# A decoder step with paged attention: the first decode sequence scored in another order, two key pages turned into a free buffer, and the last turn of the output moved by one tile

## The reference

```python
q = rms_norm((xn @ fox_w_q).reshape(B, T, H_B, HEAD_DIM), fox_q_norm)
# prompt: 256 rows attend causally to themselves
# decode sequence b: 8 rows attend to 8 cached pages of 128 rows, and to the 8 new rows
s = einsum('bqhd,bkhd->bhqk', q, k) / 8 + f_q - f_k      # masked by position
p = softmax(s); o = einsum('bhqk,bkhd->bqhd', p, v)
h = h + o.reshape(B, T, 1024) @ fox_w_o
```

## Time and profile before

| | us |
|---|---|
| median of 3 runs | 1571.27 |
| lowest and highest | 1570.28, 1572.79 |
| the profiled execution's own time | 1571.32 |
| its span in the trace | 1569.3 |
| PE busy | 1521.4 (97%) |
| DVE busy | 966.0 (62%) |
| ACT busy | 663.1 (42%) |
| projection `q` ends, attention begins (span's clock) | 1131 |
| output projection begins | 1288.7 |

### The profile page before, as it was taken

The page is one execution under the profiler, slowest core; times in us unless marked ns, Lnnn a source line. Parts: engine busy times, 40 slices in busy tenths (PEclk is TensorE's granted clock), DMA queues, the critical chain, the costliest instruction groups (busy, mean ns, idle before and its releaser), DMA issues.

```text
span 1569.3 us, 34147 instructions
## 1 busy us (share of the span) xinstructions
PE 1521.4 (97%) x14068; PEld 1420.4 (91%) x14068; DVE 966.0 (62%) x1394; ACT 663.1 (42%) x1029; POOL 125.4 (8%) x183
## 2 busy tenths in 40 slices
PE   8999999999999999999999999999988879999998
PEld 8999998998888799999999999999845549999998
DVE  6655446686897576554458655544688865655532
ACT  5443333663655653434344333333334444443321
POOL 0000000002331300000000432000012210000000
PEclk9999999999999999999999999999999999999999
DMA  8766673440010466657774554444979993444442
GB/s 267 238 213 204 223 222 106 135 135 16 17 30 10 136 204 225 226 189 228 228 240 149 180 167 142 148 148 155 376 281 408 407 367 121 135 160 137 151 148 81
DMA packets 241004, 288.54 MB, mean 184 GB/s; under 512 B 18898, under 2 KB 221922, under 8 KB 240754
## 3 DMA queue, kind: packets, MB, share of 16 engines
q1 hardware_dynamic: 237234, 281.20, 53.1%
q0 software_dynamic: 3648, 5.57, 1.4%
HBM read 280.39 MB, written 39.90 MB: 204 GB/s over the span
## 4 chain that ended last, share of the span: by engine, by line
PE 85%; DVE 9%; ACT 2%; issue 2%; DMA 1%; SPq 0%; POOL 0%; DVEq 0%
PE ps L758 24%; PE ps L759 23%; PE ps L760 23%; PE ps L1059 4%; PE ps L1054 3%; DVE ring L2841 1%; DVE ring_r L2240 1%; DMA ring<-in_fox_w_o 1%; PE ps L1511 1%; PE ps L1085 1%; PE ps L1194 1%; PE ps L1210 1%; PE ps L1149 1%; ACT ring L1882 0%; ACT ring_r L1703 0%
## 5 line engine op out<-in xcount | busy, mean ns | idle before, releaser
L758 PE MATMUL ps<-arena_r,ring_r 128*128 128x320 f32 (+1 forms) x2024 | 627.2, 310 | 0.0
L760 PE MATMUL ps<-arena_r,ring_r 128*128 128x320 f32 (+1 forms) x2024 | 624.6, 309 | 0.0
L2240 DVE TENSOR_TENSOR ring_r<-ring,ring_r 128x2048 fp32r<-128x2048 f32 (+2 forms) x131 | 291.4, 2226 | 256.8 <-ACT ring_r L1703 152.3
L758 PEld LDWEIGHTS ps<-arena_r,ring_r 128*128 128x128 f32 x2024 | 381.1, 188 | 4.1 <-issue 3.4
L760 PEld LDWEIGHTS ps<-arena_r,ring_r 128*128 128x128 f32 x2024 | 381.0, 188 | 0.0
L759 PE MATMUL ps<-arena_r,ring_r 128*128 128x320 f32 x1136 | 351.0, 309 | 0.0
L759 PE MATMUL ps<-xn_r,ring_r 128*128 128x320 f32 (+2 forms) x888 | 273.6, 308 | 0.0
L759 PEld LDWEIGHTS ps<-arena_r,ring_r 128*128 128x128 f32 x1136 | 213.3, 188 | 0.2
L2240 DVE TENSOR_TENSOR arena_r<-arena,arena_r (+3 forms) x155 | 142.2, 928 | 112.1 <-ACT arena_r L1703 50.1
L758 PE MATMUL ps<-arena_r 128*128 128x320 f32 x592 | 183.2, 309 | 0.0
L760 PE MATMUL ps<-arena_r 128*128 128x320 f32 x592 | 182.9, 309 | 0.0
(11 more groups left out here) (381 smaller groups left out, 1830.1 us busy)
## 6 DMA issues: line engine op xcount, KB each, us to landing
ring<-in_ffn_w_in SPq DMA_DIRECT2D x66, 1024.0 KB, 5.1
k_grouped<-in_cache_k SPq DMA_DIRECT2D x64, 512.0 KB, 5.4
ring<-in_ffn_w_out SPq DMA_DIRECT2D x24, 1024.0 KB, 5.1
arena<-in_cache_v SPq DMA_DIRECT2D x45, 512.0 KB, 9.4
ring<-k_grouped SPq DMA_DIRECT2D x44, 512.0 KB, 8.5
arena<-in_ffn_w_in SPq DMA_DIRECT2D x21, 1024.0 KB, 5.1
ring<-in_rw_w_rkv SPq DMA_DIRECT2D x11, 1024.0 KB, 5.1
arena<-k_grouped SPq DMA_DIRECT2D x20, 512.0 KB, 8.7
```

Of the source, the lines that this page charges most:

```text
L758: pe.matmul(out, part(s, 1)[:, k, cs], x_hi, start=first_, stop=False)
L760: return pe.matmul(out, part(s, 0)[:, k, cs], x_hi, start=False, stop=last)
L2240: return TT(out, x, high.bitcast(F32), ALU.subtract)
```

## The change

In words, for each engine:

- **Tiles.** `k_own` gets its bank before the four `q_rep` tiles. With that `q_rep` no longer occupies a bank of sequence 1's scores, and sequence 0 uses those two banks (`SCORES[1]`) for its own keys' scores and for its turned probabilities.
- **DVE.** Pages 4 and 5 of sequence 0 (unit 2) are turned into `xn`, whose content is no longer needed, so they need not wait for a scored unit: page 4 before the first `query_reciprocal`, page 5 before the mask. From unit 3 on the two buffers of `k_feat` alternate one step later. `prompt_scaled` comes after `less_max(0)`, and page 8 (the first of sequence 1) before `own_max(0)`. The steps for sequence 1 are written out: page pairs, `fox_scored(1)`, `fox_sums`, and the scaled output of sequence 0 before the last pair of pages; `less_max(1)` before `fox_scored(2)`.
- **PE.** `k_own`, units 2 and 3 and the own keys before `query_rep("q_rep")`; `fox_scores(0)` after the turned probabilities; `unit_scores(1, 2)` before `fox_values(0)`, `turn_output(0)` before `unit_scores(1, 3)`.
- **ACT.** For sequence 0 `probability_copy` before `fox_exp(0)`.
- **Output projection.** PE does the first rows of tile 1 before `turn_output(7)` instead of after it. DVE does `scaled_output(7)` before the low part of slab `fo` + 1 instead of after it.

Nothing is added to or taken from the work. The diff, shortened where a block only repeats the words above:

```diff
     add("q_own", 1, "a")
+    add("k_own", 1, "a")
     add("q_rep", DT // 2)
-    add("k_own", 1, "a")
...
-        OWN = P_TURNED[1]
+        def own_bank(b):
+            return P_TURNED[1] if b else SCORES[1][1]
         def turned(b):
-            return P_TURNED if b < BS - 1 else SCORES[(b + 1) % 2]
+            return P_TURNED if 0 < b < BS - 1 else SCORES[(b + 1) % 2]
+        def key_unit(n):
+            return xn_f[:, 0:2 * D] if n == 2 else k_feat[(n - 1) % 2 if n > 2 else n]
...
             unit_scores(0, 0)
             unit_scores(0, 1)
+            head_groups("k_own", kT)
             pe.wait_ge(S("q_rn"), 2)
+            unit_scores(0, 2)
+            unit_scores(0, 3)
+            own_scores(0)
             query_rep("q_rep", P, 2, rs[:, TS:TS + P])
-            head_groups("k_own", kT)
-            unit_scores(0, 2)
-            own_scores(0)
-            unit_scores(0, 3)
-            fox_scores(0)
...
             turn_probabilities(0)
+            fox_scores(0)
+            pe.wait_ge(S("pT_ready"), 1)
             unit_scores(1, 0)
...
+            dve_done(first["q_rep"] + 3)
             own_scores(1)
             fox_turn(1)
+            unit_scores(1, 2)
             fox_values(0)
-            unit_scores(1, 2)
+            turn_output(0)
+            unit_scores(1, 3)
             fox_scores(2)
-            unit_scores(1, 3)
-            turn_output(0)
             fox_scores(3)
...
             first_outputs(0, slice(0, T - P))
+            first_outputs(1, slice(0, T - P))
             pe.wait_ge(S("o_out"), 2 * (BS - 1))
             turn_output(b)
-            first_outputs(1, slice(0, T - P))
             split(first_slab["fo"] + 1)
...
-            for b in range(1, 5):
+            exps(0)
+            probability_copy(0)
+            fox_exp(0)
+            past_forget(1, 1)
...
-                if unit >= 2:
-                    dve.wait_ge(S("unit_scored"), unit - 1)
+                if unit >= 3:
+                    dve.wait_ge(S("unit_scored"), unit - 2 if unit < 5 else unit - 1)
...
             dve.wait_ge(dve_freed, freed["d"][first["q"] + DT])
+            turn_page(0, 4)
             query_reciprocal("q_norm_s", 0, TS)
...
             query_reciprocal("q_norm", TS, P)
+            turn_page(0, 5)
...
-            for j in range(4, PAGES):
-                turn_page(0, j)
+            turn_page(0, 6)
+            turn_page(0, 7)
             half_max(0)
-            prompt_scaled(0)
-            prompt_scaled(1)
-            prompt_scaled(2)
+            turn_page(1, 0)
             own_max(0)
-            prompt_scaled(3)
             less_max(0)
-            turn_page(1, 0)
+            for g in range(4):
+                prompt_scaled(g)
             turn_page(1, 1)
             fox_scored(0)
...
             probability_sums(b)
+            scaled_output(b)
             lo(first_slab["fo"] + 1)
-            scaled_output(b)
```

More of the change, by code:

```diff
@@ L1398, in turn_probabilities @@
             def turn_probabilities(b):
-                if b == 0:
-                    dve_done(first["q_rep"] + 3)
                 if b == BS - 1:
@@ L1506, in unit_scores @@
                               start=(j == 0), stop=False, is_transpose=True, skip_group_check=True)
-                keys = k_feat[u % 2].rearrange("p (n f x u) -> p x n f u", n=2, f=4, x=DT)
+                keys = key_unit(b * 4 + u).rearrange("p (n f x u) -> p x n f u", n=2, f=4, x=DT)
                 for e in range(2):
@@ L1524, in own_scores @@
                         x = 2 * c + e
-                        mm = mmul(ps[32 * c:32 * c + 32, OWN, 0:TS], q_cur[b % 2][:, x * 32:x * 32 + 32],
+                        mm = mmul(ps[32 * c:32 * c + 32, own_bank(b), 0:TS], q_cur[b % 2][:, x * 32:x * 32 + 32],
                                   kT[:, x, TP:T], e == 0, e == 1)
@@ L2156, in exps @@
                 own_exp(b)
-            for b in range(1, 5):
+            exps(0)
+            probability_copy(0)
+            fox_exp(0)
+            past_forget(1, 1)
+            fox_exp(1)
+            fox_columns(0)
+            fox_columns(1)
+            fox_out(0)
+            past_forget(2, 0)
+            output_columns(0)
+            for b in range(2, 5):
                 exps(b - 1)
@@ L2837, in turn_page @@
                 unit = (b * PAGES + j) // 2
-                if unit >= 2:
-                    dve.wait_ge(S("unit_scored"), unit - 1)
+                if unit >= 3:
+                    dve.wait_ge(S("unit_scored"), unit - 2 if unit < 5 else unit - 1)
                 dve.wait_ge(*k_page_in(b, j))
-                dve.transpose(k_feat[unit % 2][:, j % 2 * D:(j % 2 + 1) * D], k_page(b, j)).then_inc(S("page_turned"), 1)
+                dve.transpose(key_unit(unit)[:, j % 2 * D:(j % 2 + 1) * D], k_page(b, j)).then_inc(S("page_turned"), 1)
             def query_reciprocal(name, c0, n):
@@ L2920, in own_max @@
                     dve.wait_ge(S("p_row"), b * 3)
-                link(TT(s_new, ps[:, OWN, 0:TS], mask_new[:, b, :], ALU.add))
+                link(TT(s_new, ps[:, own_bank(b), 0:TS], mask_new[:, b, :], ALU.add))
                 dve.tensor_reduce(sst[:, 2:3], s_new, AX.X, ALU.max)
@@ L2961, in turn_pages @@
                 turn_page(b, j + 1)
-            for b in range(1, 4):
+            turn_pages(1, 2)
+            fox_scored(1)
+            fox_sums(0)
+            turn_pages(1, 4)
+            fox_sums(1)
+            probability_sums(0)
+            scaled_output(0)
+            turn_pages(1, 6)
+            half_max(1)
+            own_max(1)
+            turn_pages(2, 0)
+            less_max(1)
+            fox_scored(2)
+            fox_scored(3)
+            for b in range(2, 4):
                 turn_pages(b, 2)
-                if b == 1:
-                    fox_scored(1)
                 fox_sums(2 * b - 2)
```

## The result

The changed kernel takes 1562.69 us (median of 5 runs, 1557.42 to 1564.12), the kernel before 1571.27 (5 runs beside them); the ratio is 0.9949, with a 95% interval of 0.9931 to 0.9968. In the experiments the changed kernel was measured once more: 1561.42 us (8 runs, 1557.6 to 1564.74) against 1570.94 us, ratio 0.9939 (0.9921 to 0.9956). The forecast was 1562.4 us. Single executions of both kernels and of some variants that took far longer (1654 to 3746 us) are in no median and no ratio.

A forecast was written before the change was run, and what follows sets the result against it. PE was busy 1521.4 of 1569.3 us; the attention was paced by DVE and PE in turn and by the transfers. From 1571.3 us, 6.4 (end) plus 2.5 (front), 8.9 in all, gave 1562.4 us, range 1560.5 to 1566.5.

The forecast's parts named there:

- gain at the end: Last value page to last rows' matmuls: 6.4 us won, 4.0 of it PE's wait before `turn_output(7)`, the rest clock.
- slab `fo` + 1 in front of tile 2: Output projection: the slab's low part is ready just after PE asks for it for tile 2, a 0.1 us wait.
- page 4's cost: Sequence 0 on DVE: turning page 4 before the first reciprocal delays scaling, queries and first unit by 0.4 us.
- last value page on PE: End of the attention: the last value page's landing moves 2.5 us earlier, from 1287.5 to 1285.0 us.
- The rival of the whole half: End: all 6.83 us at 1.2 GHz give back half, 3.4 us; end 7.4, kernel 1561.4 us; chance 0.05.
- The smaller of the two shifts arrives: Attention: transfers shift by 2.5 us, DVE and PE by 3.3; only the smaller, 2.5, reaches the last value page.
- end alone: Rival: the front's gain is absorbed and only the end's 6.4 us arrives, 1564.9 us; chance 0.11.
- The slab's rival: Output projection: slab `fo` + 1 still lands at 1290.2, tile 2 waits for it, 1564.9 us; chance 0.08.
- The engines' shift: Sequence 1: DVE and PE run 3.3 us earlier than before, DVE's row at 1172.34 coming at 1169.0.
- the wait on DMA: Sign of being right: PE still waits on DMA at the last value page, near 1.4 us, before 0.65.
- The new wait: Sequence 1 on PE: `fox_scores(3)` waits some 2.2 us because `fox_scored(2)` follows `less_max(1)`; priced at nothing.
- The slower case: Rival: new waits drop the clock to 1.2 GHz in four new stretches, 1576 us; slower or nothing has chance 0.02.

The follow-up runs named there:

- the front alone: The changed kernel with its two moves in the output projection (`first_outputs(1)` on PE, `scaled_output(7)` on DVE) undone; 1567.39 us, ratio 0.9977 to the kernel before.
- the end alone: The kernel before with only the two output projection moves (`first_outputs(1)` before `turn_output(7)`, `scaled_output(7)` before the low part of slab `fo` + 1); 1564.44 us, ratio 0.9957.
- the scaling first: The changed kernel with the four prompt scalings on DVE back ahead of the maximum of sequence 0; 1567.0 us, ratio 0.9973 to the kernel before.

## Why the prediction was right

The median lies 0.3 us from the forecast. That is closer than these medians can tell, with single runs from 1557.4 to 1564.1 us, and so is partly luck; what bears the account are the steps. Point by point, with the times of the changed kernel put on the clock of the kernel before:

| step | predicted | measured |
|---|---|---|
| stretch at the end | 9.75 | 9.80, again 9.80 |
| gain at the end | 6.4 | 6.38 |
| slab `fo` + 1 in front of tile 2 | wait 0.1 | in time by 0.2 |
| page 4's cost | +0.4 | +0.39 |
| last maximum of sequence 0 ends | 1145.5 | 1145.2 |
| turned probabilities | 1146.5 | 1146.2 |
| first unit of sequence 1 | 1149.45 | 1149.2 |
| DVE's row of `fox_scored(1)` | 1153.8 | 1153.4 |
| page 24 asked for | 1156.6 | 1156.3, again 1157.3 |
| DVE's pages of sequence 1 | 1169.0 | 1168.7 |
| `fox_scores(3)` waits | 2.2 | 2.31 |
| last value page on PE | 1285.0 | 1284.4, again 1285.3 |

*The end.* The counting holds to 0.1 us. That part of the stretch at 1.2 GHz was idle and gives nothing back is shown by the front alone, where the same length with PE busy throughout costs more (3.2 us for 2.4; one trace of each). The Trainium skill, "TensorE: Matmul & The Clock Gate", section "HAM oscillation", by which the 6.83 us are worth 3.4, comes out 1.0 us too high for the kernel before and near the mark (3.4 for the 3.2 measured) where PE was busy. The rival of the whole half is refuted.

*The front.* "The smaller of the two shifts arrives" was the step that could have failed, and it held for the transfers' side. In the eight kernels that left the queue's order and its transfers alone the issue of page 24 stands at -2.8, -1.8, -2.8, -2.1, -0.5, -0.5, -0.5, +3.0 and the last page at -3.2, -2.3, -1.7, -2.5, +0.1, 0.0, -0.1, +2.3. In seven the two agree within 0.7 us; the front alone, with -2.8 and -1.7, is the exception told above. The lead at 1204 us goes from -0.6 to -6.6 and says little. The rival "end alone" (the front absorbed) falls with the changed kernel's last page at -3.2 and -2.3, against +0.1 in the kernel that has the end alone, and with the front alone, whose median is 3.5 us below the kernel before. The ratios of the changed kernel (0.9949 and 0.9939) and of the end alone (0.9957) have intervals that overlap, so that the front adds to the end is shown by these two and not by the medians of the whole change. The slab's rival falls with the stretch of 9.80.

*What was mis-sized.* The engines' shift at 1204 us was 6.6 us, or 5.5, and not 3.3, if it is counted from the trace of the kernel before. DVE's row at 1164.51 is where I had it, so the rest comes behind it: the 6.83 us at 1.2 GHz at 1174 us went as well, which I hadn't counted. But they also went in the end alone, which has the old front, so their going is not shown to be the change's doing; counted from that kernel the shift is 3.2 us, or 2.1. My 3.3 were not too small, and the trace that I forecast from had one slow stretch more than others of the same order. It changed nothing at the last page, where the transfers take such a lead back. And the wait on DMA did not grow to 1.4 us at the last page: it is 0.66 there, and the rest of the lead was handed back earlier, in the waits on value pages that the list shows. A wait at the last transfer is not the place where a lead over a saturated queue shows.

*The new wait* was priced at nothing. The one test of it, which halved it, showed no cost, and goes no further than that. The slower case found no support: stretches at half the clock in new places, which I had named as a sign of being wrong, did come, one of 3.4 us at 1163.4 (at 1132.9 and 1167.0 in the second run), but the attention has fewer of them than before.

## What to carry to other kernels

When engines and a saturated stream of transfers take turns at setting the pace, find the one issue that starts the stream, and price a reordering by how much earlier it makes that issue; a lead of the engines beyond it is given back in waits on single buffers. Then try to ask earlier in the queue, a far smaller edit than a new order of the engines. Where an engine waits behind a step that itself waits for a transfer (the scaled output behind a slab's low part here), a swap of the two is worth the wait and the clock that falls with it, and the clock's part was, in both traces that show it, about half of the busy time in the slow stretch, not half of the stretch.

## What the runs showed of the hardware

- A wait that a trace shows can go with a loss larger than itself. With the scaling first, PE waited 2.6 us longer, the clock was at 1.2 GHz for 10.2 us from 0.6 us into that wait on, and the kernel lost 5.6 us. At the end, idle times of 3.8 and 4.0 us came with a slow stretch of 6.8 us that began before they ended, and one of 0.96 us with none.
- The slow stretches come at different places in executions of one kernel: the two profiled runs of the changed kernel have them in the attention at 1163.4, and at 1132.9 and 1167.0, with the same code. Its two medians differ by 1.3 us, and single runs range from 1557.4 to 1564.7. That limits what any two of these traces can say. The kernels with the old front and all transfers as before stand from 0 to -3.4 us at 1204, those with the new order as it is in the change from -5.5 to -6.6; at the last value page they stand within 0.3 us of each other and from -1.7 to -3.2.
- Behind a saturated queue a value page lands 9.2 us after its issue in the changed kernel and 10.3 before, with the same size; with half the values in the queue before it, it lands after 3.1 us in the kernel before (that page is then half as large too). The issue of the changed kernel's last value page, at its line (median of the one):

```profile
L696 SPq DMA_DIRECT2D ring<-in_cache_v x1: 333/333/333, 1271.0 to 1271.0; - x1
...
DMA to landing us min/median/max: 9.2/9.2/9.2
```
